# First-table rows of two expert groups requested one round ahead, with a second set of row numbers, in a two-block transformer kernel

## The reference, cut to what matters

```python
s_top, i_top = lax.top_k(scores, PEER_TOPK)          # 16 of 128 keys, twice for each of 8 heads
best_s, best_pos = lax.top_k(cand_s, PEER_TOPK)      # 16 of the 256 pairs
idx = jnp.take_along_axis(cand_i, best_pos, axis=-1) # row numbers, 8 x 16 for each token
g = jax.nn.softmax(best_s, axis=-1)
h = jax.nn.gelu(jnp.einsum('td,thkd->thk', xc, u_tab[ic]), approximate=False)
return jnp.einsum('thk,thkd->td', gc * h, v_tab[ic])
```

## Time and profile before

| what | value |
|---|---|
| median of three runs | 3051.64 us (3048.47 to 3052.61) |
| the profiled run | 3052.69 us, span 3050.9 us |
| PE busy | 2737.2 us, 90% |
| DVE busy | 1679.1 us, 55% |
| ACT busy | 846.0 us, 28% |
| POOL busy | 676.8 us, 22% |
| HBM read | 835.86 MB |
| gather queue q0 | 536.90 MB |

### The profile page before, as it was taken

How to read it: one execution, slowest core, us unless ns; L and a number is a source line. 1 busy time by engine, 2 the same in 40 slices (tenths; PEclk the granted TensorE clock), 3 DMA queues, 4 the chain that set the end, 5 groups by cost and what they waited for, 6 DMA issues and landing times.

```text
span 3050.9 us, 32091 instructions
## 1 busy us (share of the span) xinstructions
PE 2737.2 (90%) x12706; PEld 1960.7 (64%) x12706; DVE 1679.1 (55%) x2521; ACT 846.0 (28%) x1237; POOL 676.8 (22%) x647
## 2 busy tenths in 40 slices
PE   8999999999999999978999877787777888777789
PEld 8999899988999887877799333333333333333347
DVE  5444555544555555444566788854555555555555
ACT  4444544433444444423554000000000100000023
POOL 0000000000000000000002555665444555454410
PEclk9999999999999999977999989999999898999999
DMA  7555555555555556442256999999999999999984
GB/s 243 165 166 166 166 185 187 181 193 193 185 187 181 192 166 215 163 105 87 84 180 224 421 421 422 420 415 422 422 422 415 422 421 422 421 422 421 422 314 147
DMA packets 229984, 839.78 MB, mean 275 GB/s; under 512 B 16215, under 2 KB 23731, under 8 KB 163812
## 3 DMA queue, kind: packets, MB, share of 16 engines
q0 software_dynamic: 73728, 536.90, 42.4%
q1 hardware_dynamic: 155084, 298.44, 30.0%
q10 hardware_dynamic: 1048, 2.70, 0.3%
HBM read 835.86 MB, written 2.13 MB: 275 GB/s over the span
## 4 chain that ended last, share of the span: by engine, by line
PE 63%; DMA 20%; DVE 7%; POOL 4%; issue 3%; ACT 2%; ACTq 0%; POOLq 0%; DVEq 0%
DMA vrows<-in_peer_u,idxc 19%; PE bank L2003 9%; PE bank L1589 8%; PE bank L1591 8%; PE bank L1592 8%; PE bank L1611 7%; PE bank L1615 7%; PE bank L1613 7%; DVE vrows L1447 4%; POOL idxc L2117 2%; POOL vrows L2126 1%; PE bank L1935 1%; PE bank L1936 1%; PE bank L1937 1%; DMA big<-in_peer_u,idxc 1%
## 5 line engine op out<-in xcount | busy, mean ns | idle before, releaser
L898 DVE TENSOR_TENSOR wl<-raw,wh 128x1024 fp32r<-128x1024 f32 (+1 forms) x544 | 653.3, 1210 | 709.5 <-ACT wh L513 709.0
L513 ACT CAST wh<-raw 128x1024 fp32r<-128x1024 f32 (+1 forms) x544 | 560.8, 1037 | 745.0 <-PE bank L1592 374.4
L1611 PE MATMUL bank<-Ah,wh 128*128 128x256 f32 x1792 | 508.7, 284 | 0.0
L1615 PE MATMUL bank<-Ah,wl 128*128 128x256 f32 x1792 | 507.3, 283 | 0.0
L1613 PE MATMUL bank<-Al,wh 128*128 128x256 f32 x1792 | 507.3, 283 | 0.0
L1447 DVE CUSTOM_DVE_ANT_0 big<-big,tmp 128x2048 f32<-128x2048 f32 x128 | 288.3, 2289 | 234.3 <-DMA big<-in_peer_u,idxc 234.3
L1447 DVE CUSTOM_DVE_ANT_0 vrows<-vrows,tmp 128x2048 f32<-128x2048 f32 x128 | 288.2, 2289 | 220.3 <-DMA vrows<-in_peer_u,idxc 220.2
L797 ACT ACTIVATE hgel<-hcur,rstd 128x2 f32<-128x2 f32 x128 | 37.7, 295 | 1188.7 <-DVE hcur L1447 1188.7
L1611 PEld LDWEIGHTS bank<-Ah,wh 128*128 128x128 f32 x1792 | 344.2, 192 | 0.4 <-issue 0.2
L1613 PEld LDWEIGHTS bank<-Al,wh 128*128 128x128 f32 x1792 | 344.2, 192 | 0.1
L1615 PEld LDWEIGHTS bank<-Ah,wl 128*128 128x128 f32 x1792 | 344.1, 192 | 0.0
(11 more groups left out here) (307 smaller groups left out, 3815.3 us busy)
## 6 DMA issues: line engine op xcount, KB each, us to landing
raw<-in_mlp_w SPq DMA_DIRECT2D x128, 1024.0 KB, 5.2
raw<-in_sb_w_qkv SPq DMA_DIRECT2D x48, 1024.0 KB, 5.2
raw<-in_w_in SPq DMA_DIRECT2D x28, 1024.0 KB, 5.1
raw<-in_sb_w_o SPq DMA_DIRECT2D x16, 1024.0 KB, 5.1
raw<-in_w_out SPq DMA_DIRECT2D x16, 1024.0 KB, 5.1
raw<-in_peer_w_q SPq DMA_DIRECT2D x16, 1024.0 KB, 5.1
raw<-in_ple_w_gate SPq DMA_DIRECT2D x16, 1024.0 KB, 5.3
tmp<-line SPq DMA_DIRECT2D x4, 768.0 KB, 6.9
```

Of the source, the lines that this page charges most:

```text
L513: nc.scalar.copy(whv[hq % 4][:, :, 0:width], raw_half[hq][:, :, 0:width]).then_inc(hi_done, 1)
L898: V_.tensor_tensor(wlv[hq % 4][:, :, 0:width], raw_half[hq][:, :, 0:width], whf[hq % 4][:, :, 0:width], ALU.subtract).then_inc(split_done, 1)
L1611: nc.tensor.matmul(o, whv[s][:, c, bs_], xh[:, kc, :], start=kc == 0 and b % 2 == 0, stop=False, skip_group_check=True)
L1615: mm = nc.tensor.matmul(o, wlv[s][:, c, bs_], xh[:, kc, :], start=False, stop=kc == KC - 1, skip_group_check=True)
```

## The change

The rows of u for groups 0 and 1 are requested one round ahead. A u buffer is no longer in use once its dots are done, so POOL now waits for `dots_done[g]` of round t and then requests the u rows of round t+1 for groups 0 and 1. Since their row numbers in `idxc` are then already those of the next round, the v rows of these two groups take theirs from a second tile, `idxv`, filled by `keep_experts`. Groups 2 and 3 are as before. The order of POOL's requests in a round becomes v0, v1, then (after waits for the dots) u0 and u1 of the next round, then u2, v2, u3, v3. The last round has nothing ahead. Rounds are now counted through both row tiles, and the waits for `idx_ready` come one round earlier, as the first numbers of a block are needed then. At the start, the v rows of group 0 are requested one by one as their buffers come free, and u rows of round 1 go between.

```diff
@@ setup
         idxc = place("idxc", GROUPS * EG, U32)[0]
+        idxv = place("idxv", 2 * EG, U32)[0]
@@ POOL
+            def take_experts(t, g):
+                nc.gpsimd.tensor_copy(idxc[:, g * EG:(g + 1) * EG], idx[:, bass.ds(t * (GROUPS * EG) + g * EG, EG)]
+                                      ).then_inc(idx_copied, 1)
+                copied()
+            def keep_experts(t, g):
+                nc.gpsimd.tensor_copy(idxv[:, g * EG:(g + 1) * EG], idx[:, bass.ds(t * (GROUPS * EG) + g * EG, EG)]
+                                      ).then_inc(idx_copied, 1)
+                copied()
+            def row_v(g, b):
+                chosen = idxv if g < 2 else idxc
...
             for g in range(2):
-                take_experts(0, 0, g)
+                take_experts(0, g)
                 rows_u(g)
-            for g in range(2):
-                pool.wait_ge(split_done, 8 * J_GATE + 4 * g + 4)
-                rows_v(g)
+                keep_experts(0, g)
+            pool.wait_ge(split_done, 8 * J_GATE + 2)
+            row_v(0, 0)
+            pool.wait_ge(split_done, 8 * J_GATE + 4)
+            row_v(0, 1)
+            pool.wait_ge(dots_done[0], EG)
+            take_experts(1, 0)
+            rows_u(0)
+            pool.wait_ge(split_done, 8 * J_GATE + 8)
+            rows_v(1)
+            pool.wait_ge(dots_done[1], EG)
+            take_experts(1, 1)
+            rows_u(1)
             pool.wait_ge(parts_used, used(J_WQ + 3))
...
-            def more_rows(m, i):
-                for g in range(GROUPS):
-                    pool.wait_ge(v_done[g], EG * m * per + EG + i * EG)
-                    take_experts(m, i, g)
+            def more_rows(t, ahead=True):
+                for g in range(2):
+                    pool.wait_ge(v_done[g], EG + t * EG)
+                    keep_experts(t, g)
+                    rows_v(g)
+                if ahead:
+                    for g in range(2):
+                        pool.wait_ge(dots_done[g], EG + t * EG)
+                        take_experts(t + 1, g)
+                        rows_u(g)
+                for g in range(2, GROUPS):
+                    pool.wait_ge(v_done[g], EG + t * EG)
+                    take_experts(t, g)
                     rows_u(g)
                     rows_v(g)
 
-            with pool.Fori(1, per // 4) as i:
-                more_rows(0, i)
+            with pool.Fori(1, per // 4 - 1) as t:
+                more_rows(t)
             pool.wait_ge(idx_ready, 2)
...
+            with pool.Fori(per + per // 2 - 1, 2 * per - 1) as t:
+                more_rows(t)
+            more_rows(2 * per - 1, ahead=False)
```

More of the change, by code:

```diff
@@ L2113, in _, with copied @@
             per = SLOTS // (GROUPS * EG)
[L2115 to L2119, removed]
+            def copied():
                 pool.wait_ge(idx_copied, 1)
                 pool.sem_clear(idx_copied)
+            def take_experts(t, g):
+                nc.gpsimd.tensor_copy(idxc[:, g * EG:(g + 1) * EG], idx[:, bass.ds(t * (GROUPS * EG) + g * EG, EG)]
+                                      ).then_inc(idx_copied, 1)
+                copied()
@@ new lines, in keep_experts, with row_u @@
+            def keep_experts(t, g):
+                nc.gpsimd.tensor_copy(idxv[:, g * EG:(g + 1) * EG], idx[:, bass.ds(t * (GROUPS * EG) + g * EG, EG)]
+                                      ).then_inc(idx_copied, 1)
+                copied()
+            def row_u(g, b):
+                nc.gpsimd.indirect_dma_start(
+                    out=ubuf[g][b], out_offset=None, in_=a["peer_u"],
+                    in_offset=bass.IndirectOffsetOnAxis(ap=idxc[:, g * EG + b:g * EG + b + 1], axis=0),
+                ).then_inc(u_landed[g], 16)
@@ L2124, in rows_u @@
+            def row_v(g, b):
+                chosen = idxv if g < 2 else idxc
+                nc.gpsimd.indirect_dma_start(
+                    out=vbuf[g][b], out_offset=None, in_=a["peer_v"],
+                    in_offset=bass.IndirectOffsetOnAxis(ap=chosen[:, g * EG + b:g * EG + b + 1], axis=0),
+                ).then_inc(v_landed[g], 16)
             def rows_u(g):
                 for b in range(EG):
[L2126 to L2129, removed]
+                    row_u(g, b)
@@ L2131, in rows_v @@
             def rows_v(g):
                 for b in range(EG):
[L2133 to L2136, removed]
+                    row_v(g, b)
             pool.wait_ge(idx_ready, 1)
             for g in range(2):
-                take_experts(0, 0, g)
+                take_experts(0, g)
@@ L2157, in _ @@
             rows_v(3)
-            def more_rows(m, i):
-                for g in range(GROUPS):
-                    pool.wait_ge(v_done[g], EG * m * per + EG + i * EG)
-                    take_experts(m, i, g)
+            def more_rows(t, ahead=True):
[11 more added lines that the diff above has]
+                    take_experts(t, g)
                     rows_u(g)
                     rows_v(g)
-            with pool.Fori(1, per // 4) as i:
-                more_rows(0, i)
+            with pool.Fori(1, per // 4 - 1) as t:
+                more_rows(t)
             pool.wait_ge(idx_ready, 2)
-            with pool.Fori(per // 4, per // 2) as i:
-                more_rows(0, i)
+            with pool.Fori(per // 4 - 1, per // 2 - 1) as t:
+                more_rows(t)
             pool.wait_ge(idx_ready, 3)
-            with pool.Fori(per // 2, per) as i:
-                more_rows(0, i)
+            with pool.Fori(per // 2 - 1, per - 1) as t:
+                more_rows(t)
             pool.wait_ge(idx_ready, 4)
-            with pool.Fori(0, per // 2) as i:
-                more_rows(1, i)
+            with pool.Fori(per - 1, per + per // 2 - 1) as t:
+                more_rows(t)
             pool.wait_ge(idx_ready, 5)
-            with pool.Fori(per // 2, per) as i:
-                more_rows(1, i)
+            with pool.Fori(per + per // 2 - 1, 2 * per - 1) as t:
+                more_rows(t)
+            more_rows(2 * per - 1, ahead=False)
 _SQUEEZE = {"x": "x", "sb_w_qkv": "sb_w_qkv", "sb_w_o": "sb_w_o", "norm_mix": "norm_mix", "norm_mlp": "norm_mlp",
```

## The result

The changed kernel takes 3133.03 us (median of 6 runs, 3125.1 to 3135.64) beside 3052.12 us for the kernel before (6 runs, 3048.47 to 3053.61): ratio 1.0263, 95% interval 1.025 to 1.0277. It is 81 us slower. The profiled run took 3132.13 us with a span of 3130.3.

A forecast was written before the change was run, and what follows sets the result against it. The prediction took the DMA to bound the expert stage at 39.8 us a round. Losses of 24.2 + 38.4 + 2.1 + 6.7 = 71.4 us less 5.1 gained took 3051.6 to 3118 us, range 3083 to 3152.

The forecast's parts named there:

- The loop: Expert stage: u3 landing, VectorE's work, POOL's request and eight rows to u3's next landing; 40.9 us steady against 39.8.
- eight rows: From POOL's first request after the dots of group 1 to u3's landing: 24.1 us, between bounds 23.3 and 24.9.
- Steady rounds: Rounds 8 to 30: 1.1 us lost in each of 22 passages from one round to the next, 24.2 us in all.
- Routing rounds: Rounds 1 to 7, with routing work between the dots: 6.4 us lost in each of six passages, 38.4 us in all.
- The second tile: Second row tile: two VectorE additions of 2.5 and 4.2 us, formerly inside waits for rows, count whole: 6.7 us lost.
- The start: Round 0 of the expert stage: four u rows put ahead fill a DMA gap, 5.1 us gained.
- nothing would be lost from 0 to 1: Passage from round 0 to round 1: the rows put ahead keep the queue full, so no loss.
- the hole: DMA idle time before the expert stage saturates, 1656 to 1676 us at share 0.41: 11.8 us.
- Dots do hold POOL: Rival: VectorE's dots delay u1's request or copy each round, 2.0 us more in 28 rounds, 3174 us; chance 0.07.
- only the routing rounds bind: Rival: steady rounds fit in 39.8 us, so mainly rounds with routing work lose; +34, 3086 us; chance 0.12.
- Faster: Rival: the DMA queue never runs down, so only the gain at the beginning shows, 3040 to 3047 us; chance 0.06.
- no change: Rival: early requests come out late and small losses in some rounds cancel, within 6 us of 3052; chance 0.03.

The follow-up runs named there:

- start-only kernel: Against the kernel before: only the change's start (early u rows of round 1), nothing ahead in round 1, old order from round 2; 3049.78 us, ratio 0.9997.

## Why the prediction was right, point by point

**The loop.** Its parts, its place and what it does were as put: eight rows behind the wait for d1, VectorE in front of it. Moving the waits took the loss away, twelve rows in place of eight made 45.0 us where 45.1 were worked out, and added VectorE work was free in the one order and paid for in the other. The terms are another matter: several were off both ways, and part of the closeness of the sum is luck.

**Steady rounds.** The term of 1.1 us a passage was too small: 1.5 over nineteen of them, or 1.6 without the one from 15 to 16. VectorE's 15.7 us were 15.9, POOL's 1.1 were 1.2. The eight rows, for which I took 24.1, the middle of 23.3 and 24.9, took 23.9 in the round shown and 25.5 in the next one (request at 2200.73, landing at 2226.18), 24.3 on average, and 23.2 to 25.6 over the steady passages. Why they differ is open. I had expected a queue that is just empty to hide some of the slow start; instead the DMA was slow in the stretch around u0 and u1. The estimate by the Trainium skill's fit (DMA: Bandwidth & Descriptors, Anatomy of one DMA) would have been further off, since it made the passages shorter.

**Routing rounds.** 38.4 us forecast for six passages, 36.2 measured, but by two errors that cancel. The loop was longer than 46.2 (46.6 on average: VectorE's part 20.7 for 21.0, the eight rows 24.6 for 24.1). And the base was not 39.8: before, these passages took 40.6, as the table shows, so there was less to lose. I had read the period from steady rounds and carried it over. Other traffic isn't behind the 0.8 us: in these six passages before, the DMA moved 102.49 MB at 421 GB/s, and 102.45 of them were the gather queue's. That is 1.7 rows more than the 96 of six rounds, so rows behind u3 had come further at the end than at the start. Why stays open.

**The second tile.** Here 6.7 us for two additions, with 3 x 1.1 for the passages 10.0, measured 15.6. For its size this is the largest miss of a term. What failed isn't VectorE's part, which sums to 54.1 us in the three passages, where 15.7 each and the 6.7 give 53.8. It is that of POOL's reaction, 5.7 us for 3.3, and of the eight rows, 76.1 for 72.3 (before, the three took 120.3, 0.9 more than 3 x 39.8, which takes a little back). In rounds 16 to 20 both requests for u0 are held by the dots of d1, so POOL reaches the wait for d1 after these are done. Round 17, DVE and then POOL:

```profile
2410.57 2.29 DVE L1448 CUSTOM_DVE_ANT_0 big<-big,tmp 128x2048 f32<-128x2048 f32 x1
```

```profile
2410.78 2.91 POOL L2134 DMA_INDIRECT big<-in_peer_u,idxc  x1 [0.80 <-POOL idxc L2123]
2414.00 1.88 POOL L2134 DMA_INDIRECT big<-in_peer_u,idxc  x1 [0.30 <-issue]
2415.88 0.28 POOL L2123 COPY idxc<-gbc 128x2 uint32 x1
2416.96 0.97 POOL L2134 DMA_INDIRECT big<-in_peer_u,idxc  x1 [0.80 <-POOL idxc L2123]
```

The dots end at 2415.08, and the request for u1 starts 1.9 us later. Why the eight rows took longer here than in other passages wasn't measured.

**The start.** 5.1 us gained was forecast; in the changed kernel it is 9.8 at the end less 5.7 and 1.7 at the start, 2.4 us, and by itself 1 us, not to be told from none. In the changed kernel the step that failed is that nothing would be lost from 0 to 1. The loop binds there already. I had put the end of d1(1) near 1710 and u3(1) at 1737; the dots end at 1713.4, as the copy behind them shows, and d3(1) starts at 1739.4:

```profile
1713.60 0.27 POOL L2123 COPY idxc<-gbc 128x2 uint32 x1 [1.58 <-DVE hcur L1448]
```

The three parts are 18.0, 1.3 and 24.7 us, together the 43.9 of the passage. Without the loop, in the start-only kernel, the gain is lost another way: I followed the hole from the landing of v1's first row to the last row of round 0 and no further. The wait for group 2's matmuls behind it was in the old trace too, covered by the very rows that the change moves.

**The rivals.** Dots do hold POOL, and this rival came true in part. In most rounds from 8 on u0's first request starts 0.01 to 0.03 us before the first dot of d1 and takes 0.97 us (2154.12 and 2154.13 in the round shown); only the second is held, 1.87 us, which lies ahead of the wait for d1 and costs nothing. In rounds 16 to 20 it starts 0.21 us behind that dot and takes 2.91 us, and the loop is 0.7 us longer each time, 3.6 us in all. I had counted on some 2 us of cover, for one request held and not two. That it wasn't so in every steady round is luck: some hundredths of a us decide it. That only the routing rounds bind was wrong, by the nineteen passages. Faster and no change fell with the loop.

The sum: 66 us forecast, 81 measured; of the 15 between, about 8 are the steady term, 6 the second tile, 3 the start, less 2 in the routing rounds.

## What to carry to other kernels

When requests are issued in order by one engine, a new wait is priced by what stands behind it: from the landing that releases it, through the work to the wait, plus all rows requested behind it up to that same landing. If this is over the time in which the DMA moves a round, it is paid for every round, even if it asks for data early and every engine has slack; here the same wait at the end of the round cost nothing. And a transfer moved forward out of a queue is no longer there to cover the wait it used to cover, so follow the queue past the hole that you fill.

## What the hardware showed that I had not expected

In the changed kernel the DMA engines count as busy while they move clearly less. Around u0 and u1, when by the order of the requests little more than these rows is queued, a share of 0.97 goes with 322 GB/s (with a full queue it is 1.01 at 422):

```profile
2196.00:2202.00 6.00, 6.00 (x15) 2.65 (x15) 4.22 (x7) 0.30 (x1) 3.01 (x3) 1.00 0.97 322
```

So over 300 us of steady rounds the share reads 1.00 and the rate 406 GB/s: the share alone would say that nothing is lost, and the rate says 4%. To tell whether a DMA stage is bound by its engines, the rate is to be read beside the share.
